# Small products of different units share the slots of the weight stream

## The reference

```python
# first block: partial rope attention with 16 heads of 64, and a Mamba-2 state-space mixer
h = rms_norm(x, g_mix[i])
q, k, v, z, xbc, dt_raw = jnp.split(h @ w_in[i], splits, axis=-1)
attn = dilated_attention(q, k, v, positions, g_q[i], g_k[i])
ssm = ssd_mixer(z, xbc, dt_raw, ...)
x = x + jnp.concatenate([attn, ssm], axis=-1) @ w_out[i]
...                                     # cross attention, MLP
# second block
xr, gr, q, k, v, qi, ki, wi, g_rnn, g_att = jnp.split(x @ w_in, SPLIT_POINTS, axis=-1)
y_rnn = rg_lru(causal_dwconv(xr, ...), ...) * jax.nn.gelu(gr)      # recurrent branch
logits = jnp.einsum('bqhd,bsd->bqhs', qi, kif) * (IDX_DIM ** -0.5) # indexer, 16 heads of 64
score = jnp.einsum('bqh,bqhs->bqs', wi, jax.nn.relu(logits))
_, idx = lax.top_k(score, topk)         # the keys that each query may attend
p = jax.nn.softmax(s, axis=-1)          # second attention: 16 heads of 128
merged = jax.nn.sigmoid(g_rnn) * y_rnn + jax.nn.sigmoid(g_att) * y_att
```

## Time and profile before

| | us |
|---|---|
| median of three runs | 2627.57 |
| the profiled execution | 2629.41 |
| its span, first to last instruction | 2627.6 |
| TensorE busy in the span | 2607.9 |
| VectorE busy | 1744.7 |
| ScalarE busy | 1333.9 |
| GpSimd busy | 79.8 |

### The profile page before, as it was taken

One profiled execution on the slowest core, in us unless ns is written; L12 is line 12 of the kernel. 1 busy time (PEld: TensorE's weight loads), 2 busy tenths in 40 slices (PEclk: granted clock), 3 DMA queues, 4 the chain that ended last, 5 costly groups with the idle time before them and its releaser, 6 DMA issues.

```text
span 2627.6 us, 50632 instructions
## 1 busy us (share of the span) xinstructions
PE 2607.9 (99%) x21444; PEld 2529.3 (96%) x21444; DVE 1744.7 (66%) x2547; ACT 1333.9 (51%) x1809; POOL 79.8 (3%) x57
## 2 busy tenths in 40 slices
PE   9999999999999999999999999999999999999998
PEld 9987898999999999999899999999999999999996
DVE  7787788765555555556787786556676656665665
ACT  6474675644443443444445774444455435543553
POOL 0000021100000000000000000000300000000001
PEclk9999999999999999999999999999999999999999
DMA  7545556466666666665554555555465565555553
GB/s 258 180 150 165 189 161 200 162 206 193 196 193 193 194 194 194 195 194 183 167 168 152 169 193 193 193 194 184 145 202 195 194 226 194 193 194 194 195 190 127
DMA packets 137170, 490.15 MB, mean 187 GB/s; under 512 B 15344, under 2 KB 17904, under 8 KB 136816
## 3 DMA queue, kind: packets, MB, share of 16 engines
q1 hardware_dynamic: 136224, 485.87, 56.7%
q10 hardware_dynamic: 720, 1.06, 0.1%
HBM read 484.77 MB, written 2.10 MB: 185 GB/s over the span
## 4 chain that ended last, share of the span: by engine, by line
PE 95%; DVE 3%; ACT 1%; DMA 0%; issue 0%; SPq 0%; ACTq 0%; DVEq 0%
PE ps L915 94%; DVE WL L2027 1%; PE ps L918 1%; DVE XL L2035 1%; ACT WH L1411 0%; DVE xg L2027 0%; DMA raw<-in_w_in 0%; DVE XL L2027 0%; DVE T L2027 0%; DVE xg L2035 0%; DVE T L2035 0%; DVE small L2035 0%; ACT P L1411 0%; PE ps L1025 0%; DVE AL L2035 0%
## 5 line engine op out<-in xcount | busy, mean ns | idle before, releaser
L2027 DVE TENSOR_TENSOR WL<-raw,WH 128x1024 fp32r<-128x1024 f32 (+1 forms) x911 | 1117.3, 1230 | 778.3 <-ACT WH L1411 778.0
L1411 ACT ACTIVATE WH<-raw 128x1024 fp32r<-128x1024 f32 (+1 forms) x911 | 961.9, 1057 | 1236.6 <-PE ps L915 1234.9
L915 PE MATMUL ps<-XH,WH 128*128 128x256 f32 (+1 forms) x4704 | 1306.6, 278 | 5.8 <-DVE WL L2027 3.3
L915 PE MATMUL ps<-XH,WL 128*128 128x256 f32 (+1 forms) x4704 | 1299.2, 276 | 0.0
L915 PE MATMUL ps<-XL,WH 128*128 128x256 f32 (+1 forms) x4704 | 1299.1, 276 | 0.0
L915 PEld LDWEIGHTS ps<-XH,WH 128*128 128x128 f32 (+1 forms) x4704 | 881.0, 187 | 11.1 <-issue 7.5
L915 PEld LDWEIGHTS ps<-XL,WH 128*128 128x128 f32 (+1 forms) x4704 | 881.1, 187 | 0.8
L915 PEld LDWEIGHTS ps<-XH,WL 128*128 128x128 f32 (+1 forms) x4704 | 881.0, 187 | 0.3
L915 PE MATMUL ps<-AH,WH 128*128 128x256 f32 x1600 | 441.8, 276 | 0.0
L915 PE MATMUL ps<-AH,WL 128*128 128x256 f32 x1600 | 441.6, 276 | 0.0
L915 PE MATMUL ps<-AL,WH 128*128 128x256 f32 x1600 | 441.6, 276 | 0.0
(11 more groups left out here) (248 smaller groups left out, 1740.5 us busy)
## 6 DMA issues: line engine op xcount, KB each, us to landing
raw<-in_w_up SPq DMA_DIRECT2D x304, 512.0 KB, 4.3
raw<-in_w_in SPq DMA_DIRECT2D x222, 512.0 KB, 3.7
raw<-in_w_down SPq DMA_DIRECT2D x216, 512.0 KB, 4.3
raw<-in_w_out SPq DMA_DIRECT2D x64, 512.0 KB, 4.2
raw<-in_w_gates SPq DMA_DIRECT2D x64, 512.0 KB, 4.3
raw<-in_w_ckv SPq DMA_DIRECT2D x16, 512.0 KB, 4.0
raw<-in_w_cq SPq DMA_DIRECT2D x8, 512.0 KB, 4.5
raw<-in_w_co SPq DMA_DIRECT2D x8, 512.0 KB, 3.5
```

Of the source, the lines that this page charges most:

```text
L915: return e.matmul(out, l, r, start=start, stop=True, skip_group_check=True)
L1411: return e.activation(out, x, func, **kw)
L2027: return e.tensor_tensor(out, a, b, op)
```

## The change

Only slots move; the arithmetic and its instructions stay the same. The units of the indexer go two to a slot, every four slots; those of the recurrent branch two to a slot; `cb_pe`/`xs_pe` two to a slot; the second attention's units, of which four stood within two neighbouring slots every eight slots, now stand two by two, four slots apart; `ssm_spread` gets a slot after `ssm_rs`; four of the eight `qk` units start one or two slots later.

```diff
     for j in range(8):
-        t = E("qkqk"[j // 2], j // 4) + 1 + 2 * (j % 2)
+        t = E("qkqk"[j // 2], j // 4) + 1 + 2 * (j % 2) + (1, 0, 2, 0)[j // 2]
...
     for g in range(4):
-        P.chain(conv + 1 + g, g, ("cb_pe", "cb_mask"), (B, ("cb", g), "cb_pe", "cb_mask"))
-        xs = P.chain(max(acs, conv + 1) + g, g, ("xs_pe", "xs_mul"), (B, ("xs", g), "xs_pe", "xs_mul"))
+        P.chain(conv + 1 + 2 * (g // 2), g, ("cb_pe", "cb_mask"), (B, ("cb", g), "cb_pe", "cb_mask"))
+        xs = P.chain(max(acs, conv + 3) + 2 * (g // 2), g, ("xs_pe", "xs_mul"), (B, ("xs", g), "xs_pe", "xs_mul"))
...
             ssm = P.chain(t + 4, u // 2, ("ssm_sq", "ssm_sum", "ssm_rs", "ssm_spread", "ssm_gain"),
-                          (T, ("ssm", u // 2), "ssm_sq", "ssm_sum"), (B, ("ssm", u // 2), "ssm_sum", "ssm_gain"))
+                          (T, ("ssm", u // 2), "ssm_sq", "ssm_sum"), (B, ("ssm", u // 2), "ssm_sum", "ssm_gain"),
+                          apart=("ssm_spread",))
...
-        t = P.chain(max(E("qi", 1) - 2 + 2 * u, qi + 1 if u > 5 else 0), u, ("ix_qk", "ix_relu", "ix_acc"), *bufs)
+        t = P.chain(max(E("qi", 1) - 2 + 4 * (u // 2), qi + 1 if u > 5 else 0), u, ("ix_qk", "ix_relu", "ix_acc"), *bufs)
...
-        t = P.chain(t + 2, u, steps, (B, ("lru", 2 * u), "lru_pe", "lru_tanh"), (B, ("lru", 2 * u + 1), "lru_pe", "lru_tanh"),
+        t = P.chain(t + 3 - u % 2, u, steps, (B, ("lru", 2 * u), "lru_pe", "lru_tanh"), (B, ("lru", 2 * u + 1), "lru_pe", "lru_tanh"),
...
     for h in range(16):
-        t = head_steps(P, 12 + h, max(t, E("q2", h // 4) + 3 + (h // 2) % 2))
+        t = head_steps(P, 12 + h, max(t, E("q2", h // 4) + 3 + 4 * (h // 2 % 2)))
         out2.append(t)
-        t += -7 + 2 + h % 2
+        t += -7 + h % 2
```

## The result

The changed kernel takes 2637.88 us (median of 6, 2637.16 to 2638.75) against 2627.93 for the kernel before on the same chip (6 runs, 2627.55 to 2629.68). The ratio is 1.0036 [1.0025, 1.0046]: slower by 0.36%, some 10 us. The forecast was 2634.3 with a range of 2629.5 to 2641. So the sign and the range held, and the time came out 3.6 above the forecast. It lies near the value of the rival in which the clock falls once (2637).

A forecast was written before the change was run, and what follows sets the result against it. TensorE, busy 99% of the span, was taken to bound the kernel. Terms -1.65, -1.2, -0.25, +1.55, +7.8 and +0.5 sum to +6.75 us, taking 2627.57 to 2634.3 us; range 2629.5 to 2641.

The forecast's parts named there:

- the rival in which the clock falls once: Second attention: TensorE's new waits halve its clock; one fall gives 2636 to 2638 us, three up to 2644.5; chance 0.28.
- The main step: Second attention, slots 478, 486, 494: `sm_norm` queues behind `rq` 4 and 5 on VectorE, TensorE waits; +7.8 us.
- The sum per slot: Second attention: TensorE loses 2.6 us in each of slots 478, 486 and 494.
- the forecast's upper bound: Second attention, three slots: 3 x 2.85 = +8.6 us, with a restart after each wait.
- the overhead of a group of 64-row products: Indexer: about 0.41 us paid once per group, so four pairs of units save 1.65 us.
- the waits of the earlier trace: State-space stretch: TensorE's waits of 0.58 and 0.33 us for `ssd_mask` and `ssm_rs` go, with restarts -1.2 us.
- the wait for `sm_norm` 3: First attention, slot 88: TensorE waits 0.7 us before `sm_tr` 3; part of +1.55 us.
- the one for `qk_gain` 5: First attention, before the second v chunk: TensorE waits 0.85 us more; part of +1.55 us.
- Full-width products: Second attention, recurrent gates, `xs`, `cb`: joining groups shares no overhead, 0 us, bound -0.5.
- the first two cases: Clock stays up in the new waits, 2634.3 us, chance 0.50; or it falls there, 2637 us, chance 0.28.

The follow-up runs named there:

- the fill: Changed kernel with five products of constants on TensorE ahead of the wait in slots 478, 486 and 494: 2636.26 us, ratio 1.0029.

## Why the prediction was right, and where it was short

The main step held: the new slots put `sm_norm` of one pair in each of three slots behind both `rq` on VectorE. The forecast gave 7.00 for the end of `rq` 5, 7.7 for the first normalisation and waits of 2.2 and 0.35. The trace has 7.00, 7.74, and, counted from start to start as the forecast did, waits of 2.24 and 0.27. (In brackets stands 2.08, which counts from the modelled end of the product before; so counted, the second is 0.11.) The sum per slot came out a little larger (2.63 to 2.70 instead of 2.6): behind each wait the second transpose starts 0.17 after the first instead of 0.11, which is the restart that the forecast's upper bound had named, and in slots 486 and 494 the wait itself is 2.31. Swapping the two loops took the loss away, which shows that the position in VectorE's queue is the cause. The rule of the Trainium skill weighed in the forecast (TensorE: Matmul & The Clock Gate, "Architectural detail: the array is 16× 32×32, not 1× 128×128"), strict first in, first out on VectorE, is what these rows show: `RECIPROCAL` at 1366.19, right behind the last `rq` instruction at 1365.58 and not one place ahead of it.

The smaller terms held within 0.15 each: the overhead of a group of 64-row products is paid once (-1.5 to -1.6 for -1.65), the waits of the earlier trace rows went (-1.31 for -1.2), and both the wait for `sm_norm` 3 and the one for `qk_gain` 5 came, as one sum (+1.61 for +1.55). Counted from start to start the two are 0.65 and 0.81 for 0.7 and 0.85 (0.48 and 0.65 in brackets), with the restarts making up the rest. Full-width products and the recurrent branch moved nothing.

What was short is the choice between the first two cases. The forecast took the clock to stay up in the new waits, at 0.50 against 0.28 for its rival, since the mean grant was 0.997 and had stayed up through the waits of the earlier trace rows. Those waits were 0.58 and 0.33 long, about a quarter of the new ones or less, and said little about a wait of 2.1 with only transposes behind it. Of the rows it had, was the better guide: there TensorE ran nothing wide, and the grant was 0.50. The runs put one fall of 3.4 us and about 1.6 into each profile with the three waits, the fill takes it out, and this is the rival's case of one fall, as it was worked out: 2636 to 2638. With it the sum is 6.75 + 1.7 = 8.5 for about 8.7 by the traces. So the range held, but the forecast's own sum fell 3.2 short of the 9.95 between the medians: 1.6 of it is the fall that the sum had left out, 0.3 the sizes of the other terms, and 1.2 is not explained. Part of that may lie in the layer norm's low clock, which varies, and which no run takes apart for the median.

## What to carry to other kernels

Where an engine walks a fixed order of steps, moving a step by slots also moves it past every other step of its new slot: before a chain is moved, list what stands ahead of it in the queue there, when that work can start, and whether the engine has any idle time left in the stretch. A saving on the busiest engine from sharing a slot is small and sure (0.4 us per joined pair of 64-row groups); a producer that lands behind a late one on another engine costs 2.6 us each time, and can be mended by the order in the slot without giving up the slots. Price a new wait of some us on TensorE with a clock fall as well.

## What the runs showed of the hardware

A wait of TensorE of 2.1 us, followed by six transposes and then wide products at once, preceded one fall of the granted clock to 0.50 for 3.4 us in each of four profiles (three at full clock otherwise, one at 0.95), though the same wait stood there three times; the slot differed between two executions of one kernel (486 and 478). With five products of constants in place of the idle time, and the same transposes behind them, no fall came in the one profile taken. The layer norm's low clock, with nothing changed in it, was absent, 3.4 or 6.8 us long from one execution to the next. The stretch took 12.6 us without it, 12.9 to 13.1 with 3.4 us and 14.3 to 14.7 with 6.8, so that spans of this kernel differ by up to some 2 us for no cause of their own.
